# Gated delta rule, state scan: output products grouped by their number of weight rows, latent key and value tiles moved between the chunks

## The reference, cut to what matters

```
v_new = u_n - w_n @ state
o     = (q_n * exp(g_n)) @ state  +  a_n @ v_new
state = state * exp(g_last) + (k_n * exp(g_last - g_n)).T @ v_new
```

```
kv = rmsnorm(mkv) @ w_ukv        # 256 -> 8 heads x (128 key + 128 value columns)
```

## Time and profile before

| | |
|---|---|
| runs (three) | 2407.71 us median, 2407.62 to 2413.1 |
| profiled execution, its own time | 2406.57 us |
| its span | 2404.8 us |
| mean granted TensorE clock | 0.958 of full speed |
| PE busy | 2272.4 us, 94% of the span |
| PEld busy | 1578.5 us |
| DVE busy | 1242.5 us |
| ACT busy | 878.1 us |
| POOL busy | 609.0 us |

### The profile page before, as it was taken

The page is one execution under the profiler, slowest core; times in us unless marked ns, Lnnn a source line. Parts: engine busy times, 40 slices in busy tenths (PEclk is TensorE's granted clock), DMA queues, the critical chain, the costliest instruction groups (busy, mean ns, idle before and its releaser), DMA issues.

```text
span 2404.8 us, 24775 instructions
## 1 busy us (share of the span) xinstructions
PE 2272.4 (94%) x9464; PEld 1578.5 (66%) x9464; DVE 1242.5 (52%) x1866; ACT 878.1 (37%) x1372; POOL 609.0 (25%) x282
## 2 busy tenths in 40 slices
PE   8999899988999899979989999999899899999997
PEld 4777765665777656656758765665477587666654
DVE  5677744516687645326598523332246885133321
ACT  4333354334323353334543313342236433133421
POOL 3223320333233221234322100113234230001220
PEclk9999999998999999998989989999999899989998
DMA  6313321422323211322220011122322100111221
GB/s 210 109 60 101 99 71 48 140 76 79 101 70 105 93 62 53 122 101 70 73 61 27 18 35 45 44 70 93 105 70 81 56 24 23 38 37 44 79 79 53
DMA packets 46732, 175.97 MB, mean 73 GB/s; under 512 B 5394, under 2 KB 6162, under 8 KB 45208
## 3 DMA queue, kind: packets, MB, share of 16 engines
q1 hardware_dynamic: 46520, 174.26, 22.8%
q10 hardware_dynamic: 96, 0.13, 0.0%
HBM read 159.69 MB, written 14.68 MB: 73 GB/s over the span
## 4 chain that ended last, share of the span: by engine, by line
PE 74%; DVE 22%; ACT 2%; issue 2%; DMA 0%; DVEq 0%; ACTq 0%
PE bank L552 12%; PE bank L561 12%; PE bank L566 11%; PE bank L622 4%; PE bank L762 4%; PE bank L986 4%; PE bank L575 2%; PE bank L946 2%; PE bank L634 2%; PE bank L960 2%; DVE arena L1473 2%; PE bank L945 1%; DVE rs L1461 1%; PE bank L610 1%; PE bank L702 1%
## 5 line engine op out<-in xcount | busy, mean ns | idle before, releaser
L2033 POOL TENSOR_TENSOR w_lo<-wraw,w_hi 128x1024 fp32r<-128x1024 f32 (+1 forms) x206 | 505.3, 2454 | 1570.5 <-ACT w_hi L1008 1570.5
L1008 ACT ACTIVATE w_hi<-wraw 128x1024 fp32r<-128x1024 f32 (+1 forms) x206 | 216.6, 1051 | 777.4 <-PE bank L566 452.0
L552 PE MATMUL bank<-h_hi,w_hi 128*128 128x512 f32 x1648 | 454.4, 417 | 38.2 <-ACT h_hi L1020 30.4
L552 PEld LDWEIGHTS bank<-h_hi,w_hi 128*128 128x128 f32 x1648 | 311.0, 192 | 168.5 <-issue 82.7
L561 PE MATMUL bank<-h_lo,w_hi 128*128 128x512 f32 x1648 | 410.7, 391 | 0.5 <-POOL h_lo L2029 0.5
L566 PE MATMUL bank<-h_hi,w_lo 128*128 128x512 f32 x1584 | 391.4, 389 | 0.0
L561 PEld LDWEIGHTS bank<-h_lo,w_hi 128*128 128x128 f32 x1648 | 311.1, 189 | 69.2 <-POOL h_lo L2029 0.9
L566 PEld LDWEIGHTS bank<-h_hi,w_lo 128*128 128x128 f32 x1584 | 296.1, 187 | 63.1
L1461 DVE RECIPROCAL rs<-rs 128x512 f32<-128x512 f32 x17 | 57.0, 3353 | 172.6 <-ACT rs L1033 172.6
L622 PE MATMUL bank<-arena,wdir 128*128 128x512 f32 x256 | 114.3, 598 | 0.0
L986 PE MATMUL bank<-arena,wdir 128*128 128x512 f32 x256 | 112.4, 592 | 0.0
(11 more groups left out here) (316 smaller groups left out, 3103.4 us busy)
## 6 DMA issues: line engine op xcount, KB each, us to landing
wraw<-in_w_split SPq DMA_DIRECT2D x204, 512.0 KB, 3.5
wdir<-in_w_direct SPq DMA_DIRECT2D x52, 512.0 KB, 3.6
x_park<-arena SPq DMA_DIRECT2D x3, 2048.0 KB, 6.2
arena<-x_park SPq DMA_DIRECT2D x3, 2048.0 KB, 7.9
hg_park<-arena SPq DMA_DIRECT2D x2, 2048.0 KB, 9.2
arena<-hg_park SPq DMA_DIRECT2D x2, 2048.0 KB, 9.0
arena<-bias_rows SPq DMA_DIRECT2D x2, 1792.0 KB, 7.5
arena<-in_xT SPq DMA_DIRECT2D x2, 1024.0 KB, 7.1
```

Of the source, the lines that this page charges most:

```text
L552: mm(ps[0:wd, 0:S], hi[:, k, :].bitcast(F32R), h_hi[:, k, :].bitcast(F32R), start=k == 0 and not begun, stop=False)
L1008: a(w_hi[:, n % 2, 0:f].bitcast(F32R), wraw[:, n % 2, 0:f], ACT.Copy).then_inc(hi_done, 1)
L2033: nc.gpsimd.tensor_tensor(w_lo[:, n % 2, 0:f].bitcast(F32R), wraw[:, n % 2, 0:f], w_hi[:, n % 2, 0:f], ALU.subtract).then_inc(lo_done, 1)
```

## The change

Four things are changed, all in the second block, in both layers.

1. In a chunk, `oc` is taken before `su`. Its four state products (128 weight rows) are issued right behind `qn`, ahead of the wait for `vnew`; its four `vnew` products (64 weight rows) come behind `su`. Only the first product of the bank starts the accumulation, only the last ends it.
2. Behind `oc`, each chunk now has one latent tile: `kn` 0 to 3 in chunks 0 to 3, `vv` 0 to 3 in chunks 4 to 7. The tiles 4 to 7 of both stay behind the scan. ACT copies each moved tile behind its `oc` copy.
3. `per` of `kn` and `vv` goes from 4 to 2.
4. TensorE's wait for the normed `ckv` stands ahead of the scan.

```diff
+BESIDE_STATE = [[("kn", n)] if n < 4 else [("vv", n - 4)] for n in range(NC_)]
@@ psum_plan
-            jobs += [("vn", l, ck), ("qn", l, ck)] + ([("su", l, ck)] if ck < NC_ - 1 else []) + [("oc", l, ck)]
-        jobs += [("kn", l, h) for h in range(MH)] + [("on", l)]
-        jobs += [("vv", l, h) for h in range(MH)] + [("nb", l, h) for h in range(H)]
+            jobs += [("vn", l, ck), ("qn", l, ck), ("oc", l, ck)] + ([("su", l, ck)] if ck < NC_ - 1 else [])
+            jobs += [(g, l, j) for g, j in BESIDE_STATE[ck]]
+        jobs += [("kn", l, h) for h in range(4, MH)] + [("on", l)]
+        jobs += [("vv", l, h) for h in range(4, MH)] + [("nb", l, h) for h in range(H)]
@@ weight_chunks
-    per = {"pa": 2, "ph": 2, "qr": 2, "qn": 2, "kn": 4, "vv": 4}
+    per = {"pa": 2, "ph": 2, "qr": 2, "qn": 2, "kn": 2, "vv": 2}
@@ TensorE
+                def values_tile(h):
+                    ps = take("vv", l, h)
+                    w = direct_w(("vv", l, h - h % 2), 2)
+                    for tt in range(NT):
+                        for k in range(2):
+                            ins = mm(ps[:, tt * P:(tt + 1) * P], ckv[:, k, tt * P:(tt + 1) * P], w[:, h % 2, k, :],
+                                     start=k == 0, stop=k == 1)
+                    ins.then_inc(filled("vv", l, h), 1)
...
+                pe.wait_ge(*after("ckv_norm", l, 1))
...
                     tile("qn", ck)
+                    out = take("oc", l, ck)
+                    for h in range(H):
+                        mm(out[:, h * CH:(h + 1) * CH], st[:, ck % 2, h, :], qg[:, h, ck * CH:(ck + 1) * CH],
+                           start=h == 0, stop=False)
                     pe.wait_ge(*read("vn", l, ck))
                     if ck < NC_ - 1:
                         ps = take("su", l, ck)
...
-                    ps = take("oc", l, ck)
                     for h in range(H):
-                        mm(ps[:, h * CH:(h + 1) * CH], st[:, ck % 2, h, :], qg[:, h, ck * CH:(ck + 1) * CH],
-                           start=True, stop=False)
-                        ins = mm(ps[:, h * CH:(h + 1) * CH], vnew[part, tt % 2, h, :], dtm[part, tt, h, part],
-                                 start=False, stop=True)
+                        ins = mm(out[:, h * CH:(h + 1) * CH], vnew[part, tt % 2, h, :], dtm[part, tt, h, part],
+                                 start=False, stop=h == H - 1)
                     ins.then_inc(filled("oc", l, ck), 1)
+                    for g, j in BESIDE_STATE[ck]:
+                        if g == "vv":
+                            values_tile(j)
+                        else:
+                            tile(g, j)
-                pe.wait_ge(*after("ckv_norm", l, 1))
-                for h in range(MH):
+                for h in range(4, MH):
                     tile("kn", h)
@@ ScalarE
                     act.wait_ge(*read("oc", l, ck))
+                    for g, j in BESIDE_STATE[ck]:
+                        keep((g, l, j), (kn if g == "kn" else vn)[:, j, :])
...
-                for h in range(MH):
+                for h in range(4, MH):
                     keep(("kn", l, h), kn[:, h, :])
                 row_root(("on", l), row_q, P)
-                for h in range(MH):
+                for h in range(4, MH):
                     keep(("vv", l, h), vn[:, h, :])
```

More of the change, by code:

```diff
@@ L757, in tile @@
                         return
-                    per, kt, src = {"qn": (2, 3, cq), "qr": (2, 3, cq), "kn": (4, 2, ckv)}[g]
+                    per, kt, src = {"qn": (2, 3, cq), "qr": (2, 3, cq), "kn": (2, 2, ckv)}[g]
                     ps = take(g, l, j)
@@ L914, in _ @@
                         ins.then_inc(filled("su", l, ck), 1)
-                    ps = take("oc", l, ck)
                     for h in range(H):
-                        mm(ps[:, h * CH:(h + 1) * CH], st[:, ck % 2, h, :], qg[:, h, ck * CH:(ck + 1) * CH],
-                           start=True, stop=False)
-                        ins = mm(ps[:, h * CH:(h + 1) * CH], vnew[part, tt % 2, h, :], dtm[part, tt, h, part],
-                                 start=False, stop=True)
+                        ins = mm(out[:, h * CH:(h + 1) * CH], vnew[part, tt % 2, h, :], dtm[part, tt, h, part],
+                                 start=False, stop=h == H - 1)
                     ins.then_inc(filled("oc", l, ck), 1)
-                pe.wait_ge(*after("ckv_norm", l, 1))
-                for h in range(MH):
+                    for g, j in BESIDE_STATE[ck]:
[4 more added lines that the diff above has]
+                for h in range(4, MH):
                     tile("kn", h)
                 row_sums(("on", l), [onsq[:, h, :] for h in range(H)], [("on_sq", l, h) for h in range(H)])
-                for h in range(MH):
[L928 to L934, removed]
+                for h in range(4, MH):
+                    values_tile(h)
                 for h in range(H):
```

## The result

The changed kernel takes 2391.16 us (median of 4 runs, 2388.75 to 2392.37), the kernel before on the same occasion 2410.4 (4 runs, 2407.62 to 2413.14). The ratio is 0.9919, with a 95% interval of 0.9904 to 0.9934: 19 us faster. A later series gave 0.9925 (0.9906 to 0.9944). The forecast was 2377 with a range of 2371 to 2392. The measured time lies at the slow edge of that range and outside the 2371 to 2382 to which the forecast itself gave 0.74: 19 of the 31 us came.

What follows compares the result with a forecast made beforehand. TensorE's own pace was taken to bound the scan. Grouping (16.8 us) plus clock (14.6) less load waits (0.6) gave 30.8 us off 2406.57, 2375.8; the median lies 1.1 above, so 2377, range 2371 to 2392.

Steps and rivals of the forecast that it cites:

- Price of a change of weight rows, pace in a group: In the scan's chunks: 0.14 us per row change, 0.11 us per grouped record; 16.8 us less in two layers.
- Rule of the Trainium skill on weight loads: For grouped `oc` records: loads overlap only matmuls of different row groups, so most of 16.8 us would go; small chance.
- Latent tile as cover for the state: Ahead of the next `vn`: the tile hides the new state with 1.0 us to spare; without it, 0.7 us late.
- Cover of the rows for `nb`: Behind the scan: four value tiles give 7.2 us against 6.0 needed from `on` to ready rows; cost zero.
- Loads: Weight loads for two tiles: hidden except at `kn` 6, late by 0.2 to 0.4 us; 0.6 us more in two layers.
- Clock in the scans: Both scans: TensorE's clock falls end because the stretch of `oc` ahead of them no longer exists; 14.6 us less.
- The sum: Whole kernel: 16.8 + 14.6 - 0.6 = 30.8 us off the profiled 2406.57, so 2375.8, and 2377 as median.
- the clock still falls: Rival, in the scans: with all falls kept 2391.5 us, with half 2384; chance 0.18 for anything from 2382 up.

Runs made afterwards that it cites:

- the four groups: Kernel before, `oc` in its old place but its products in four groups of four records: 2402.18 us, ratio 0.9963.
- the grouping alone: Changed kernel with output products grouped, but all eight latent tiles behind the scan and loads of four as before: 2412.7 us, ratio 1.0008.
- the tiles alone: Changed kernel with latent tiles between chunks and loads of two, but output products head by head behind `su` as before: 2431.65 us, ratio 1.0082.
- the fastest version: Changed kernel with `on` between `kn` 5 and `kn` 6, value tiles 6 and 7 in the latent attention's first two steps: 2368.85 us, ratio 0.9824.

## Why the prediction was right, and where it fell short

- *Price of a change of weight rows, pace in a group* (0.14 us, 0.11 us): the pace is right, and so is the sum. A chunk takes 8.47 us for 8.43. The places are not: `qn` to the state products takes 2.68 us for 2.57 forecast, these to `su` 0.93 for 1.02, `su` to the `vnew` products 0.99 for 0.88, those to the tile 0.93 for 1.02. The two changes of rows that are left cost 0.05 us each, and two places costed without a change cost 0.11 each. That these offset each other is luck. The price of 0.14 is shown by the four groups, where it holds.
- *Rule of the Trainium skill on weight loads* ("TensorE: Matmul & The Clock Gate", Part 3, "What overlaps and what doesn't": a load overlaps a matmul in flight only if their row groups differ): the trace does not agree. Eight loads on the same rows, beside matmuls on those rows, took 0.97 us in the group of L932.
- *Latent tile as cover for the state*: right, and shown by its absence: 0.82 to 0.85 us of waiting per chunk without it. The prediction says 0.7; its own terms, 2.8 less 0.88 + 1.02, give 0.9.
- *Cover of the rows for `nb`*, in the timeline behind the first scan (`kn` 4 and 5, `kn` 6 and 7, `on`, the value tiles, the last of DVE's rows, `nb`):

```profile
1444.94 3.67 PE L764 MATMUL bank<-arena,wdir 128*128 128x512 f32 x8
...
1449.18 3.67 PE L764 MATMUL bank<-arena,wdir 128*128 128x512 f32 x8 [0.57 <-DMA wdir<-in_w_direct]
...
1452.78 3.60 PE L786 MATMUL bank<-arena,onecol 128*4 128x512 f32 x8
...
1456.31 7.41 PE L777 MATMUL bank<-wdir,arena 128*128 128x128 f32 x64
...
1461.73 0.68 DVE L1782 TENSOR_TENSOR rows<-rs,rows 4x512 fp32r<-4x512 f32 x1
...
1463.65 1.20 PE L769 MATMUL bank<-rows,sel 36*128 36x512 f32 x4
```

  Right. The rows are ready at 1462.41, `nb` starts at 1463.65.
- *Loads*: the place was right (`kn` 6), the size a little low: 0.57 + 0.34 = 0.9 us for 0.6. From issue to the waiting product this load takes 4.07 us in the first layer (1445.11 to 1449.18) and 3.74 in the second, not 3.6.
- *Clock in the scans*, 14.6 us: came in full, seven falls to none. My reason, that the interleaved `oc` makes the clock fall and its removal ends that, is only half of it: with the grouping alone it fell in three chunks of seven. So the second largest term of the sum came out right by more than its reason gives, and that much is luck.
- *What fell short* is "The sum": it took the clock outside the scans as it stood in one profile, without a term or a bound for it. That profile had 307 us in the latent attentions and none of the falls in the first block; the changed kernel's had 312.8 and about 6 us there. In place of 30.8 us the two profiles differ by 29.3 - 5.8 - 6.1 + 0.4 = 17.8. The rival "the clock still falls" had the right size (2384 to 2391.5, measured 2391.16) and the wrong place: it looked for the falls in the scans. The slow edge of the range was set for that rival, so that the measured time lies inside it is luck. How much of the loss belongs to the version stays open: the kernel before shows both losses too, once 1.8 us of work per layer is added, but over all runs the gain is 18 to 19 us and not 29, so the changed kernel meets such losses more often. In which stretch its other runs and those of the kernel before meet them is not shown, for only two of each were profiled.

## What to carry to other kernels

Products with different numbers of weight rows should stand in groups, and the time that interleaving them had covered must be given other work: here the grouping alone gained nothing in the whole time (11 us in its stretch), the tiles alone lost 20 us, and both together gained 19 (29 in their stretch). On a kernel whose TensorE is near half clock in places, read the granted clock by stretch in more than one execution before adding up a gain, for a later stage can give a third of it back. Idle steps at the head of a softmax loop can take independent tiles: in the fastest version two tiles lengthened them by 1.1 us for 3.6 us of work. What that gives in all has to be measured for each version, for the same two tiles gained 3.5 us in the kernel before, and a third one lost 12.

## What was not expected of the hardware

- TensorE's clock fell with TensorE busy for all of the time: 0.82 over 9.40 busy us of 9.40. What ran ahead of the fall was `oc`, short products with a change of rows every 0.36 us; the instructions that became longer were the `vn` and `qn` behind it. Dense groups of equal products (67 us of scan and tiles) stayed at 1.00.
- With 3.6 us of dense work added to the kernel before, its one run was 20.8 us longer than the profiled one without (2428.46 for 2407.67): 5.2 in scans and tiles, 11.8 in the latent attentions, 4.5 ahead of the first scan, where nothing had been added. The kernel before itself ran up to 2421.65, so how much of it the added work brings is not shown.
- The fall pattern in the first seven chunks of the scan of before is the same in both layers and in all four profiles that have this scan (chunks of some 8.2, 10.6, 7.8, 7.8, 9.4, 7.8, 9.4 us, to 0.2), though the first scan begins up to 8 us later. There the clock follows the code and not the moment.
